# Rows of 320 values for the split activations, and the other buffers placed anew

## What is computed

```
first block:   h = norm(x) * (1 + scale) + shift;  q, k, v, gates = h @ w_in
               x += gate * (attention(16 heads) @ branches * gates) @ w_out
               x += gate * relu(norm2(x) @ w_mlp_in)^2 @ w_mlp_out;  x = norm(x) * final_g
second block:  x = [meta tokens, x]
  layer 0:     x += 0.5 * swiglu(norm(x));  x += pool_mixer(norm(x));  x += 0.5 * swiglu(norm(x))
               k, v = up(norm(norm(x) @ w_dkv))          (shared keys and values)
  layer 1:     x += 0.5 * swiglu(norm(x));  x += latent attention(norm(x), k, v);  x += 0.5 * swiglu(norm(x))
out = norm(x), without the meta tokens
```

## Time and profile before

| | |
|---|---|
| median of three runs | 1235.67 us |
| the profiled execution's own time | 1234.03 us |
| its span, first to last instruction | 1232.3 us |
| granted TensorE clock, mean | 0.998 |
| TensorE busy | 1208.6 us, 98% |
| VectorE busy | 862.2 us, 70% |
| ScalarE busy | 633.9 us, 51% |
| GpSimd busy | 172.2 us, 14% |
| DMA | 239.17 MB, mean 194 GB/s |

### The profile page before, as it was taken

How to read it: one execution, slowest core, us unless ns; L and a number is a source line. 1 busy time by engine, 2 the same in 40 slices (tenths; PEclk the granted TensorE clock), 3 DMA queues, 4 the chain that set the end, 5 groups by cost and what they waited for, 6 DMA issues and landing times.

```text
span 1232.3 us, 23766 instructions
## 1 busy us (share of the span) xinstructions
PE 1208.6 (98%) x9956; PEld 1185.4 (96%) x9956; DVE 862.2 (70%) x1214; ACT 633.9 (51%) x985; POOL 172.2 (14%) x178
## 2 busy tenths in 40 slices
PE   6999999999999999999999999999999999999997
PEld 4999999999999999999999999999999988999996
DVE  6789888776756766556766656766666777766654
ACT  6557546675545444434544444454444567544541
POOL 3024323000322000012200001320001221000021
PEclk9999999999999999999999999999999999999999
DMA  9997775667564555654455565456556533555551
GB/s 361 321 338 269 240 251 172 240 235 261 168 220 154 177 172 172 204 173 136 124 185 171 172 204 173 148 180 201 177 191 200 188 120 95 203 199 177 191 164 35
DMA packets 67563, 239.17 MB, mean 194 GB/s; under 512 B 7380, under 2 KB 9573, under 8 KB 67456
## 3 DMA queue, kind: packets, MB, share of 16 engines
q1 hardware_dynamic: 66800, 235.41, 57.2%
q0 software_dynamic: 656, 2.24, 0.5%
HBM read 236.55 MB, written 1.07 MB: 193 GB/s over the span
## 4 chain that ended last, share of the span: by engine, by line
PE 93%; DVE 2%; issue 0%; ACT 0%; POOL 0%; DVEq 0%
PE G L611 28%; PE G L610 28%; PE G L612 28%; PE A L610 1%; PE A L612 1%; PE A L611 1%; DVE sb_wlo L1568 0%; PE A L762 0%; PE A L1056 0%; PE A L777 0%; PE A L750 0%; PE G L1111 0%; PE G L1112 0%; PE G L1113 0%; PE A L1090 0%; PE A L640 0%
## 5 line engine op out<-in xcount | busy, mean ns | idle before, releaser
L1568 DVE TENSOR_TENSOR sb_wlo<-sb_raw,sb_whi 128x1024 fp32r<-128x1024 f32 (+1 forms) x398 | 487.9, 1258 | 77.4 <-ACT sb_whi L1169 77.3
L610 PE MATMUL G<-sb_xh,sb_whi 128*128 128x256 f32 (+2 forms) x1752 | 496.5, 283 | 0.4 <-DVE sb_wlo L1568 0.4
L611 PE MATMUL G<-sb_xl,sb_whi 128*128 128x256 f32 (+2 forms) x1752 | 496.8, 284 | 0.0
L612 PE MATMUL G<-sb_xh,sb_wlo 128*128 128x256 f32 (+2 forms) x1752 | 495.1, 283 | 0.0
L1169 ACT ACTIVATE sb_whi<-sb_raw 128x1024 fp32r<-128x1024 f32 (+1 forms) x397 | 404.5, 1045 | 175.5 <-PE G L612 156.9
L610 PEld LDWEIGHTS G<-sb_xh,sb_whi 128*128 128x128 f32 x1752 | 329.7, 188 | 0.9 <-DVE sb_wlo L1568 0.7
L612 PEld LDWEIGHTS G<-sb_xh,sb_wlo 128*128 128x128 f32 x1752 | 329.3, 188 | 0.0
L611 PEld LDWEIGHTS G<-sb_xl,sb_whi 128*128 128x128 f32 x1752 | 329.2, 188 | 0.0
L610 PE MATMUL G<-sb_hh,sb_whi 128*128 128x256 f32 (+1 forms) x1056 | 296.0, 280 | 1.5 <-DVE sb_hh L1809 1.4
L612 PE MATMUL G<-sb_hh,sb_wlo 128*128 128x256 f32 (+1 forms) x1056 | 296.1, 280 | 0.0
L611 PE MATMUL G<-sb_hl,sb_whi 128*128 128x256 f32 (+1 forms) x992 | 279.0, 281 | 0.0
(11 more groups left out here) (335 smaller groups left out, 1225.2 us busy)
## 6 DMA issues: line engine op xcount, KB each, us to landing
sb_raw<-in_wstream SPq DMA_DIRECT2D x438, 512.0 KB, 4.4
sb_raw<-in_wstream SPq DMA_DIRECT2D x8, 320.0 KB, 7.6
sb_bias<-bias_scratch POOLq DMA_DIRECT2D x1, 2048.0 KB, 16.8
sb_X<-in_xT SPq DMA_DIRECT2D x2, 512.0 KB, 5.1
out_T<-sb_X SPq DMA_DIRECT2D x4, 256.0 KB, 2.7
sb_con<-in_consts SPq DMA_DIRECT2D x1, 601.0 KB, 10.1
sb_band<-in_bands SPq DMA_DIRECT2D x1, 314.0 KB, 5.1
sb_vec<-in_vecs SPq DMA_DIRECT2D x1, 82.5 KB, 2.0
```

Source lines behind the costliest of these rows:

```text
L610: e.matmul(out, w_h, xs, start=k0 + s.kt == 0, stop=False)
L611: e.matmul(out, w_h, xr, start=False, stop=False)
L612: m = e.matmul(out, w_l, xs, start=False, stop=k0 + s.kt == ktotal - 1)
L1568: e.tensor_tensor(wlo[:, i % NSPLIT, 0:w], raw[:, c % NRAW, 0:w], f(whi[:, i % NSPLIT, 0:w]), ALU.subtract).then_inc(lo_done, 1)
```

## The change

Rows of xh and xl get 320 places, of which 272 or 258 are used; the tokens' 256 columns stay at columns 16 to 271 where only these are used, and the 272 columns begin at column 16 (`wide`), with the meta tokens at 16 to 31. The two shift columns of mlp_in stand behind the tokens, at 272 and 273, and their results are read from there. Hidden rows of 272 columns get 320 places each (`hid_cols`), those of 256 keep theirs. Of the eight rows of the keys' input three stay behind the hidden rows, and five go to new buffers `kin_h` and `kin_l`, which share the place of `oh`, `ol`.

To make room, the table of ones is cut to 312 values (its third constant is used in one column alone), and `band` moves to the place of `oh`. Its DMA therefore waits for the end of the product that reads `oh` last (`brb3`) and is issued ahead of the first chunk of `mlp_in4`. `sq` moves ahead of `raw`, a pad of 32 values goes, and `cqh`, `cql` change places with a gap. The names of steps, the loops, and the order of work on the engines stay as they are.

```
-        xh, xl = sb("xh", [P, KT, T], F32R), sb("xl", [P, KT, T], F32R)
+        xh, xl = sb("xh", [P, KT, ROW], F32R), sb("xl", [P, KT, ROW], F32R)
+        sq = sb("sq", [P, 2, T])
...
-        mean_ones = sb("mean_ones", [P, 3, P])
-        sumsq, sumsq2, sq = sb("sumsq", [P, T]), sb("sumsq2", [P, T]), sb("sq", [P, 2, T])
+        mean_ones = sb("mean_ones", [P, 2 * P + 56])
+        sumsq, sumsq2 = sb("sumsq", [P, T]), sb("sumsq2", [P, T])
...
-        band = sb("band", [P, BANDC])
...
-        sb("pad", [P, 32])
...
+        with ExitStack() as s:
+            band = sb("band", [P, BANDC], to=s)
+        with ExitStack() as s:
+            kin_h, kin_l = sb("kin_h", [P, KT - KIN, ROW], F32R, to=s), sb("kin_l", [P, KT - KIN, ROW], F32R, to=s)
         oh, ol = sb("oh", [P, 8, SEQ], F32R), sb("ol", [P, 8, SEQ], F32R)
...
-        kvx = FF2 * T
+        kvx = FF2 * ROW
...
-        SHIFT = slice(META - 2, T)
+        SHIFT = slice(META, T + 2)
+        wide = lambda cols: slice(cols.start + META, cols.stop + META)
...
-        kvcols = lambda kt: slice(kvx + kt * T, kvx + (kt + 1) * T)
+        kvcols = lambda kt: slice(kvx + kt * ROW, kvx + kt * ROW + T)
+        kv_high = lambda kt: hh[:, kvcols(kt)] if kt < KIN else kin_h[:, kt - KIN, ALL]
...
+        hid_cols = lambda f_, j: slice(j * ROW, j * ROW + T) if FFN_COLS[f_] == ALL else slice(j * SEQ, (j + 1) * SEQ)
...
-                if c == where["wout0"][0][0]:
+                if c == where["mlp_in4"][0][0]:
+                    e.wait_ge(mm_done, ended["brb3"])
                     e.dma_start(band[:, :], bands).then_inc(band_in, 16)
...
-                src = lambda kt: (xh[:, kt, cols], xl[:, kt, cols])
+                at = wide(ALL) if cols == ALL else cols
+                src = lambda kt: (xh[:, kt, at], xl[:, kt, at])
...
-                hid = lambda kt: (hh[:, kt * n:(kt + 1) * n], hl[:, kt * n:(kt + 1) * n])
+                hid = lambda kt: (hh[:, hid_cols(f_, kt)], hl[:, hid_cols(f_, kt)])
...
-                e.tensor_copy(shift_out[:, b, :], g[:, :, 0])
+                e.tensor_copy(shift_out[:, b, :], g[:, :, SEQ])
                 e.wait_ge(rstd_done, RSTD["norm2"])
-                e.tensor_tensor(hf(i), g[:, :, 2:2 + SEQ], rb, ALU.mult).then_inc(left_dve, 1)
+                e.tensor_tensor(hf(i), g[:, :, 0:SEQ], rb, ALU.mult).then_inc(left_dve, 1)
```

More of the change, by code:

```diff
@@ L511, in build_program @@
         COLS1, ALL = slice(META, T), slice(0, T)
-        SHIFT = slice(META - 2, T)
+        ones_of = lambda which: mean_ones[:, which * P:min((which + 1) * P, 2 * P + 56)]
+        SHIFT = slice(META, T + 2)
+        wide = lambda cols: slice(cols.start + META, cols.stop + META)
         REV = lambda ap: ap[:, :, ::-1]
@@ L639, in mean @@
                 for k, part in enumerate(parts):
-                    m = e.matmul(A[bank][:, 0:n], mean_ones[:, which, :], part, start=k == 0, stop=k == len(parts) - 1)
+                    m = e.matmul(A[bank][:, 0:n], ones_of(which), part, start=k == 0, stop=k == len(parts) - 1)
                 m.then_inc(mean_done, 1)
@@ L905, in mix @@
                     for out, a, m in zip(outs, (META, META + P, 0), (P, P, META)):
-                        x_h, x_l = xh[:, 2 * gi + kt, a:a + m], xl[:, 2 * gi + kt, a:a + m]
+                        x_h, x_l = (x[:, 2 * gi + kt, wide(slice(a, a + m))] for x in (xh, xl))
                         opens = gi % 2 == 0 and kt == 0
@@ L919, in token_means @@
                 for n, a in enumerate((META, META + P, 0)):
-                    m = e.matmul(A[0][:, n:n + 1], sumsq[:, a:a + P], mean_ones[:, 0, 0:1], start=True, stop=True)
+                    m = e.matmul(A[0][:, n:n + 1], sumsq[:, a:a + P], ones_of(0)[:, 0:1], start=True, stop=True)
                 m.then_inc(mean_done, 1)
@@ L1012, in query_means @@
                     cols = slice(META + n * P, META + (n + 1) * P)
-                    m = e.matmul(A[0][:, n:n + 1], sumsq[:, cols], mean_ones[:, 0, 0:1], start=True, stop=True)
+                    m = e.matmul(A[0][:, n:n + 1], sumsq[:, cols], ones_of(0)[:, 0:1], start=True, stop=True)
                 m.then_inc(mean_done, 1)
@@ L1016, in query_means @@
                     for kt in range(QR):
-                        m = e.matmul(A[1][:, n:n + 1], cqf[:, kt, n * P:(n + 1) * P], mean_ones[:, 2, 0:1], start=kt == 0, stop=kt == QR - 1)
+                        m = e.matmul(A[1][:, n:n + 1], cqf[:, kt, n * P:(n + 1) * P], ones_of(2)[:, 0:1], start=kt == 0, stop=kt == QR - 1)
                 m.then_inc(mean_done, 1)
@@ L1150, in tensor_program @@
             e.wait_ge(sumsq_done, SUMSQ["ffn2_1"] - 1)
-            e.matmul(out, mean_ones[:, 0, :], sumsq[:, COLS1], start=True, stop=False)
+            e.matmul(out, ones_of(0), sumsq[:, COLS1], start=True, stop=False)
             e.wait_ge(sumsq_done, SUMSQ["ffn2_1"])
-            e.matmul(out, mean_ones[:, 0, :], sq[:, LAST_SQ, COLS1], start=False, stop=False)
+            e.matmul(out, ones_of(0), sq[:, LAST_SQ, COLS1], start=False, stop=False)
             e.wait_ge(last_square, 1)
-            e.matmul(out, mean_ones[:, 0, :], sq[:, 1 - LAST_SQ, COLS1], start=False, stop=True).then_inc(mean_done, 1)
+            e.matmul(out, ones_of(0), sq[:, 1 - LAST_SQ, COLS1], start=False, stop=True).then_inc(mean_done, 1)
         def scalar_program(e):
@@ L1625, in residual, with x_lo @@
                                            ALU.mult, ALU.add).then_inc(left_dve, 1)
-            def x_lo(stage, i, cols, gain):
+            def x_lo(stage, i, cols, gain, at=None):
+                at = at or cols
                 for t in range(2):
```

47 lines of the change are left out of this document (25 added, 22 removed).

## The result

The changed kernel takes 1236.32 us (median of 20 runs, 1234.3 to 1237.8); the kernel before, measured beside it, 1234.62 (1233.39 to 1235.68). The ratio is 1.0016, with a 95% interval of 1.001 to 1.0022: a little slower, just inside the 0.2% that the prediction called no change. The forecast was 1218 us.

A forecast was written before the change was run, and what follows sets the result against it. TensorE's matmul stream, busy 1208.6 of 1232.3 us, was taken as the bound. Terms 5.2 + 7.6 + 3.5 + 0.5 = 16.8 us less than 1234.0 gave 1217.2, or 1218.8 from the median; forecast 1218, range 1206 to 1237.

The forecast's parts named there:

- What bounds the kernel: Whole kernel: TensorE is busy 1208.6 of 1232.3 us, so almost only a faster stream of matmuls can shorten the run.
- that the place of the rows sets the spacing: Matmul stream: the operand rows' distance from the weight buffers, modulo 256 bytes, sets the time; 113.5, 117.8 and 120.0 ns seen.
- 272 columns, 5.2 us less: First feed-forward block's and other 272-column products, 3264 matmuls: 125.0 to 123.4 ns each, 5.2 us less.
- 256-column gate/up, 116.9 to 113.3, 7.6 us less: Gate/up of two feed-forward blocks, 2112 matmuls: all at distance 192 in its fast cycle, 7.6 us less; slow cycle 1.9 more.
- mlp_out and the down products unchanged: mlp_out and the last two blocks' down products stay at distance 192: nothing gained; in the slow cycle 8.2 us more.
- slower rival: Slow cycle takes all long 256-column stages, mlp_out and down products included: 1240 us; chance 0.08.
- rival of the slow blocks: One or both 256-column blocks settle in the slow cycle, gate/up and down products: 1225 or 1232 us; chance 0.25.
- mlp_in, 115 ns: mlp_in's 768 matmuls of 258 columns move to distance 192: from 119.6 to 115 ns, 3.5 us less.
- Gate products, 0.5 us less: Attention stage's 384 gate products, short runs starting anew, half in either cycle: 115.5 ns, 0.5 us less.
- Band table, other engines: Band table's DMA, moved and waiting for brb3, costs nothing; VectorE, ScalarE and GpSimd do the same work: no new bound.
- rival "no change": Whole kernel: the place decides otherwise than by distance, so the time stays 1234 to 1237 us; chance 0.11.
- A: The experiments' theory: distance 192 has two cycles at 256 columns, the way in decides; shifting both operands changes nothing.

The follow-up runs named there:

- Experiment 1: Separate kernel without the model: TensorE alone multiplies constant buffers in stretches of one operand distance; 256 columns at 192 took 113.4 or 117.8 ns after a pause.
- the first map: Constant-buffer stretches with TensorE alone, entered from a pause or another distance; at distance 192, 13 of 19 entered from a pause ended at 113.3 ns, 6 at 117.8.
- experiments 5: Against the six-idle-matmul kernel, four in ffn1_1 and ffn2_1: 1223.39 us. Against the changed kernel, weights at distance 112: 1255.87; with mlp_in at 16 besides: 1253.09.
- 7: Against the changed kernel, 256-column blocks' rows 44 values later (distance 112): 1223.06 us. Against the 6, 4, 4 idle-matmul kernel, mlp_in's rows at distance 16: 1219.94.
- experiment 3: Against the changed kernel: all buffers 128 bytes higher, 1236.71 us; separately, rows of ffn1_1, mix1 and ffn2_1 stepping by 272 values again, 1231.11 us.
- after: The kernel with the change, against the kernel before it: 1236.32 us, ratio 1.0016.

## Why the prediction was wrong, point by point

- **What bounds the kernel** and **that the place of the rows sets the spacing**: right. Experiment 1 gives the same spacings with every other engine at rest. The Trainium skill's rule that the prediction set against it (TensorE: Matmul & The Clock Gate, "Step-by-step: what each phase is for": loading the next weights takes no read bandwidth from the running matmul) doesn't hold for this stream in the sense that the prediction gave it, that the place decides nothing: at one size and one clock, 113.3 to 121.7 ns at 256 columns by the operands' places. SBUF — State Buffer, "Who interferes with whom", says that PE waits on no other engine; with that the runs agree, since with the others stopped the spacings were the same (113.3, 117.8 and 120.0 ns).
- **272 columns, 5.2 us less**: right, 5.1 measured; 123.3 for 123.4 ns.
- **256-column gate/up, 116.9 to 113.3, 7.6 us less**: the step that failed. The prediction had seen both cycles at 192 and chose the fast one, because "where a stream came from other distances it went to the fast one". That was true of before, and it is the very thing that the change takes away: with one distance for all, no product hands over from another distance any more. Starts behind a stop, a mean or a transpose stay where they fall, slow in 6 of 19 behind a stop in the first map, and nothing puts them right later. The term came out at 1.4 us more in place of 7.6 less. With another way in (experiments 5 and 7) the term is there: 885 in 100 us.
- **mlp_out and the down products unchanged**: failed by the same step. They were fast in before because the products ahead of them ended at another distance. Putting the steps back showed it for the down products; for mlp_out the six matmuls at 128 showed that the way in decides, and that its old way in from mlp_in did it is inferred. The term came out at 6.1 us more in place of nought; the prediction's slower rival had this mechanism at 8.2 us and gave it 0.08, and its rival of the slow blocks, at 0.25, had the blocks' part of it.
- **mlp_in, 115 ns**: a size taken from a neighbour. No row showed 258 columns at 192, and I bounded them by 256 columns scaled (114.2 to 118.7); they take 120.8 there, outside both bounds, and the term was +1.0 us and not -3.5.
- **Gate products, 0.5 us less**: not read apart. The whole stretch up to mlp_in came out 0.2 us longer, with the longer waits of the start in it.
- **Band table, other engines**: right. SyncE issues mlp_in4's first load at 202.78 us, 0.26 later than before, as mlp_in began 0.22 later. TensorE has no new wait for VectorE; the one for the first split of the input was 1.4 us longer, at the start.
- **The number**: that 1236.3 us lies in the stated range (1206 to 1237) is luck. It is outside the forecast's own 1212 to 1223, and it is the time of the rival "no change" (1234 to 1237, given 0.11) without that rival's reason: distance did decide, and a gain at 272 columns met a loss at 256.

With the fast cycle put in place by four and six idle matmuls the kernel takes 1223.4 us, 10.8 less than the one before measured beside it (1234.2), where the sum had 16.8. Of the missing 6.0, mlp_in's term is 4.5, and the 14 idle matmuls themselves are an estimated 1.6 (14 x 113.3 ns). What stays open: which reads collide inside the memory, the reason for the 32 bytes, and what makes one start behind a stop fall into the slow cycle and another not. With constant buffers, the first stretch of each run left out, the slow cycle was met at shifts of 0 and 192 only (10 of 19 starts behind a pause), and in none of 24 at the six other multiples of 32. So the place weighs the odds there, against what A expected; it doesn't settle them, for in the model the slow cycle stood at a shift of 128 too (experiment 3).

## What to carry to other kernels

A stream that alternates weight loads and matmuls can have more than one steady rate at the same sizes and addresses, so a row that shows a rate shows one cycle and not the price; ask how the stream entered it, and what in the old layout kept kicking it. Making addresses uniform takes such kicks away. Where the last few per cent of such a stream matter, measure the spacing of the exact column count at the exact distance with constant buffers (three short runs did it here), choose a distance that settles from every entry, and keep the weight tiles at the alignment at which it was measured (here multiples of 32 bytes, for 256 columns).

## What the runs showed of the hardware that was not expected

- One 256-column matmul with its own weight load took 113.3 to 121.7 ns at a granted clock of 1.00, by the places of its operands (113.3, 116.7, 117.8, 118.7 and 120.0 among others); one stretch ran at 130.0. The Trainium skill (TensorE: Matmul & The Clock Gate, "Back-to-back issue gap") gives N / 2.4 + 2.5 ns as the gap of an isolated matmul, which would be an estimate of 109.2 at 256 columns, and says that in a stream of weight loads and matmuls this counts too little at small N and too much at large N. Here it counts too little: no stretch with constant buffers settled under 113.3.
- The best distance depends on the column count: 192 and 112 at 256 columns, 112, 140, 160, 176, 188 and 192 at 272 (123.3 ns), 16 at 258 (116.7). Two columns more than 256 cost 7.5 ns at 192 (113.3 to 120.8), and no stretch of 258 there came under 120.
- At distance 192 in after the slow cycle lasted for the 528 matmuls of each down product, window after window, and for nearly all 1056 of each gate/up.
- Two idle matmuls more or less in each of two blocks were worth 13.5 us.
